# A down projection whose hidden tiles are taken in chunks of six, eight and eight instead of eight, eight and six

## What is computed

```python
    hf = rms_norm(x, g_ffn)
    x = x + (jax.nn.silu(hf @ w_gate) * (hf @ w_up)) @ w_down
y_prompt = rms_norm(xp, g_final)
y_sample = rms_norm(xs, g_final)
```

## Time and profile before

| | |
|---|---|
| median of three runs | 803.87 us (803.01, 804.04, 803.87) |
| profiled execution | 803.4 us |
| its span, first to last instruction | 801.4 us |
| TensorE matmuls, busy | 783.0 us |
| VectorE, busy | 570.8 us |
| ScalarE, busy | 454.3 us |
| GpSimd, busy | 450.8 us |
| granted TensorE clock, mean share of full | 0.996 |

### The profile page before, as it was taken

How to read it: one execution, slowest core, us unless ns; L and a number is a source line. 1 busy time by engine, 2 the same in 40 slices (tenths; PEclk the granted TensorE clock), 3 DMA queues, 4 the chain that set the end, 5 groups by cost and what they waited for, 6 DMA issues and landing times.

```text
span 801.4 us, 16035 instructions
## 1 busy us (share of the span) xinstructions
PE 783.0 (98%) x5731; PEld 744.6 (93%) x5731; DVE 570.8 (71%) x1058; ACT 454.3 (57%) x865; POOL 450.8 (56%) x351
## 2 busy tenths in 40 slices
PE   7999999999999999999999999999999999999996
PEld 6987998888888999998899999999999999899996
DVE  6446477887779736457589777667676689998884
ACT  7462475666677334454465655555555566555464
POOL 3666873383213554741465454454674588889954
PEclk9999999999999999999999999999999999999998
DMA  8343432111025333340023233223332232232213
GB/s 258 115 124 108 155 92 79 36 34 41 28 79 176 128 106 105 106 132 28 18 96 107 97 106 105 71 86 105 105 105 66 91 106 84 76 106 88 81 45 119
DMA packets 26538, 75.93 MB, mean 95 GB/s; under 512 B 2912, under 2 KB 7464, under 8 KB 26344
## 3 DMA queue, kind: packets, MB, share of 16 engines
q1 hardware_dynamic: 25920, 74.28, 28.9%
q10 hardware_dynamic: 560, 0.88, 0.3%
HBM read 68.62 MB, written 6.53 MB: 94 GB/s over the span
## 4 chain that ended last, share of the span: by engine, by line
PE 86%; DVE 4%; issue 3%; ACT 3%; POOL 2%; DMA 1%; SPq 0%; POOLq 0%; DVEq 0%; ACTq 0%
PE ps L1179 13%; PE ps L652 13%; PE ps L1181 13%; PE ps L1180 13%; PE ps L654 12%; PE ps L653 12%; PE ps L814 2%; PE ps L832 2%; PE ps L670 1%; PE ps L1084 1%; ACT whi L1318 1%; DMA wraw<-w_front 1%; POOL wlo L2611 1%; PE ps L678 1%; PE ps L797 1%
## 5 line engine op out<-in xcount | busy, mean ns | idle before, releaser
L1318 ACT ACTIVATE whi<-wraw 128x512 fp32r<-128x512 f32 (+3 forms) x150 | 112.7, 755 | 91.5 <-PE ps L1181 43.4
L652 PE MATMUL ps<-hhi,whi 128*128 128x288 f32 x480 | 144.6, 301 | 5.9 <-DVE hlo L1877 5.8
L2762 POOL TENSOR_TENSOR wlo<-wraw,whi 128x512 fp32r<-128x512 f32 x63 | 86.2, 1381 | 106.5 <-ACT whi L1318 106.5
L654 PE MATMUL ps<-hlo,whi 128*128 128x288 f32 x480 | 143.0, 298 | 0.0
L653 PE MATMUL ps<-hhi,wlo 128*128 128x288 f32 x480 | 142.9, 298 | 0.0
L2611 POOL TENSOR_TENSOR wlo<-wraw,whi 128x256 fp32r<-128x256 f32 (+2 forms) x83 | 90.9, 1123 | 84.9 <-ACT whi L1318 84.7
L1179 PE MATMUL ps<-hhi,whi 128*128 128x288 f32 x380 | 112.2, 295 | 1.1 <-DVE xb L2480 0.6
L1180 PE MATMUL ps<-hhi,wlo 128*128 128x288 f32 x380 | 111.9, 295 | 0.0
L652 PEld LDWEIGHTS ps<-hhi,whi 128*128 128x128 f32 x480 | 91.2, 190 | 7.5 <-DVE hlo L1877 5.8
L1181 PE MATMUL ps<-hlo,whi 128*128 128x288 f32 x320 | 94.4, 295 | 0.0
L653 PEld LDWEIGHTS ps<-hhi,wlo 128*128 128x128 f32 x480 | 91.2, 190 | 0.2
(11 more groups left out here) (383 smaller groups left out, 2261.6 us busy)
## 6 DMA issues: line engine op xcount, KB each, us to landing
wraw<-w_ff SPq DMA_DIRECT2D x44, 512.0 KB, 4.1
wraw<-w_front SPq DMA_DIRECT2D x41, 512.0 KB, 3.7
wraw<-w_down SPq DMA_DIRECT2D x16, 512.0 KB, 4.1
wraw<-w_down SPq DMA_DIRECT2D x8, 384.0 KB, 3.5
wraw<-w_front SPq DMA_DIRECT2D x7, 384.0 KB, 3.8
xa<-x_t SPq DMA_DIRECT2D x8, 288.0 KB, 5.6
xs<-x_t SPq DMA_DIRECT2D x7, 288.0 KB, 5.7
out_y<-xb SPq DMA_DIRECT2D x5, 288.0 KB, 2.6
```

What stands on the lines that cost most here:

```text
L652: nc.tensor.matmul(out, lh, rh, start=start, stop=False)
L654: return nc.tensor.matmul(out, lh, rl, start=False, stop=stop)
L1318: return nc.scalar.activation(out, src, func, **kw)
L2762: g.tensor_tensor(w_operand(1, j), src, f(w_operand(0, j)), ALU.subtract).then_inc(g_lo, 1)
```

## The change

The chunks become 6, 8 and 8 tiles. Stage 0's weights are still prepared in blocks of 512 columns, of which 384 are the stage's own, so its load places each block of 384 columns at a distance of 512. The places of hidden operands (`D_HI`) and the uses that they wait for (`D_PLACE`) follow the new sizes, and so do the counts of scaled tiles (6, 14, 22). Squares at the end lie in tiles 6 and up. `hidden_scaled(20)` goes from VectorE's stage 1 to GpSimd, behind `down_rest(1, 1)`. The last column sums of the second half take tile 13, then `sqacc`, then tile 12. Core of the diff:

```diff
@@ -43,7 +43,7 @@
 B_FRONT = 49
 BLOCK_COLS = [768 if b < 4 or b in B_UQ else 1024 for b in range(B_FRONT)]
 BLOCK_AT = [sum(BLOCK_COLS[:b]) for b in range(B_FRONT + 1)]
-DOWN_K = (8, 8, 6)
+DOWN_K = (6, 8, 8)
 
 
 TICKS = 80
@@ -467,19 +467,19 @@
 
         D_SRC = [turns(c, True) for c in range(3)]
         D_LO = [turns(c, False) for c in range(3)]
-        D_HI = [{0: pb[:, :, :], 2: hlo[:, 0:4, x_low], 1: th[0][:, :, :], 4: tl[0][:, :, :], 3: hhi[:, 4:8, x_low],
-                 5: hlo[:, 4:8, x_low], 6: th[2][:, :, :]},
+        D_HI = [{0: pb[:, 0:3, :], 2: hlo[:, 0:3, x_low], 1: th[0][:, 0:3, :], 4: tl[0][:, 0:3, :], 3: hhi[:, 4:7, x_low],
+                 5: hlo[:, 4:7, x_low], 6: th[2][:, 0:3, :]},
                 {0: hhi[:, 0:4, x_high], 2: hlo[:, 0:4, x_high], 1: hhi[:, 4:8, x_high], 4: hlo[:, 4:8, x_high],
                  3: pb[:, :, :], 5: hlo[:, 0:4, x_low], 6: pa[:, :, :]},
-                {0: tl[0][:, 0:3, :], 2: hhi[:, 4:7, x_low], 1: hlo[:, 4:7, x_low], 4: th[2][:, 0:3, :], 3: hidlo[:, 0:3, x_low],
-                 5: hidlo[:, 4:7, x_low], 6: hidlo[:, 0:3, x_high]}]
+                {0: tl[0][:, :, :], 2: hhi[:, 4:8, x_low], 1: hlo[:, 4:8, x_low], 4: th[2][:, :, :], 3: hidlo[:, 0:4, x_low],
+                 5: hidlo[:, 4:6, :].rearrange("p k (h t) -> p (k h) t", h=2), 6: hidlo[:, 0:4, x_high]}]
         T_PLACE = [{5: ff_used(G, 0)}, {4: ff_used(G, 4), 2: ff_used(G, 3), 5: ff_used(G, 3)}, {4: used_at(3, 4), 2: used_at(3, 5), 5: used_at(3, 1)}]
         D_PLACE = [{2: ff_used(G, 0), 1: ff_used(G, 2), 4: ff_used(G, 2), 3: ff_used(G, 1), 5: ff_used(G, 1),
                     6: ff_used(G, 4)},
                    {0: ff_used(G, 5), 2: ff_used(G, 5), 1: ff_used(G, 6), 4: ff_used(G, 6), 3: used_at(3, 0), 5: used_at(3, 2),
                     6: used_at(3, 2)},
-                   {0: used_at(3, 4), 2: used_at(3, 3), 1: used_at(3, 5), 4: used_at(3, 6), 3: used_at(3, 0), 5: used_at(3, 1),
-                    6: used_at(3, 3)}]
+                   {0: used_at(3, 4), 2: used_at(3, 3), 1: used_at(3, 5), 4: used_at(3, 6), 3: used_at(3, 1), 5: used_at(3, 6),
+                    6: used_at(3, 6)}]
 
         def down_w(s):
 
@@ -501,7 +501,8 @@
         def down_raw(s, r, k):
 
             w = down_w(s)
-            return w_raw((NW + s, None))[:, r, w * k:w * k + w]
+            at = 512 * k if s == 0 else w * k
+            return w_raw((NW + s, None))[:, r, at:at + w]
 
         def down_loaded(eng, s):
 
@@ -1280,8 +1281,8 @@
 
             def last_columns(half):
 
-                sources = ((hidf[:, 15, :], e_sq, 4), (hidf[:, 14, :], e_sq, 4), (sqacc[:, 0:T], e_acc, 5)) if half == 0 else \
-                    ((sqacc[:, 0:T], e_acc, 7), (hidf[:, 15, :], e_sq, 6), (hidf[:, 14, :], e_sq, 7))
+                sources = ((hidf[:, 13, :], e_sq, 4), (hidf[:, 12, :], e_sq, 4), (sqacc[:, 0:T], e_acc, 5)) if half == 0 else \
+                    ((hidf[:, 13, :], e_sq, 6), (sqacc[:, 0:T], e_acc, 7), (hidf[:, 12, :], e_sq, 7))
                 for n0, (source, signal, count) in enumerate(sources):
                     after(pe, signal, count)
                     for n in range(LAST_N):
@@ -1713,7 +1714,7 @@
                 if j in TURNS:
                     turns_made(act, c, TURNS[j])
                 else:
-                    act.wait_ge(s_hsc, (8, 16, 22)[c])
+                    act.wait_ge(s_hsc, (6, 14, 22)[c])
                 if j in D_PLACE[c]:
                     act.wait_ge(g_used, D_PLACE[c][j])
                 activation(D_HI[c][j], D_SRC[c][j]).then_inc(h_hi[0], 1)
@@ -1771,7 +1772,7 @@
 
             def pair_squares(b):
                 after(act, d_vec, vec_at(8 + b, "x7"))
-                activation(hidf[:, 8 + 2 * b:10 + 2 * b, :], xb[:, 2 * b:2 * b + 2, :], ACT.Square).then_inc(e_sq[0], 1)
+                activation(hidf[:, 6 + 2 * b:8 + 2 * b, :], xb[:, 2 * b:2 * b + 2, :], ACT.Square).then_inc(e_sq[0], 1)
 
             def gains_on(m, cols):
                 activation(xb[:, m, cols], xb[:, m, cols], scale=gains[:, G_FIN + m:G_FIN + m + 1]).then_inc(s_xg, 1)
@@ -1779,7 +1780,7 @@
             def half_squares(m0, m1, cols, names):
                 for s, name in names:
                     after(act, d_vec, vec_at(s, name))
-                activation(hidf[:, 8 + m0:8 + m1, cols], xb[:, m0:m1, cols], ACT.Square).then_inc(e_sq[0], 1)
+                activation(hidf[:, 6 + m0:6 + m1, cols], xb[:, m0:m1, cols], ACT.Square).then_inc(e_sq[0], 1)
 
             window((0, None))
             with act.Fori(0, NW // 2 - 2) as i:
@@ -1837,7 +1838,7 @@
 
             def last_row(half):
                 act.wait_ge(n_row, 7 + 2 * half)
-                activation(hidf[:, 8 + half, 0:HT], ps[:, 1 + 3 * half, 0:HT]).then_inc(n_rs, 1)
+                activation(hidf[:, 6 + half, 0:HT], ps[:, 1 + 3 * half, 0:HT]).then_inc(n_rs, 1)
 
             last_root(0)
             half_squares(4, 6, x_high, ((LA, "x7"),))
@@ -2539,7 +2540,6 @@
                 x6(s)
                 if s == 1:
                     hidden_turn(1, 2)
-                    hidden_scaled(20)
                 elif s == 2:
                     hidden_low(1, 4)
                 elif s == 3:
@@ -2765,7 +2765,7 @@
 
                 src = D_SRC[c]
                 if j == 4:
-                    pool.wait_ge(s_hsc, (8, 16, 22)[c])
+                    pool.wait_ge(s_hsc, (6, 14, 22)[c])
                     a, b = quarter(hidf, c, 0, x_high), src[0]
                 elif j == 3:
                     turns_made(pool, c, 1)
@@ -2807,7 +2807,7 @@
                     g.tensor_tensor(lo[:, 0:2, :], src[:, 0:2, :], hi[:, 0:2, :], ALU.subtract)
                 op_low(0, p)
                 if n == NW:
-                    g.tensor_tensor(lo[:, 2:4, :], src[:, 2:4, :], hi[:, 2:4, :], ALU.subtract).then_inc(h_lopool[0], 1)
+                    g.tensor_tensor(lo[:, 2:D_KN[0], :], src[:, 2:D_KN[0], :], hi[:, 2:D_KN[0], :], ALU.subtract).then_inc(h_lopool[0], 1)
                 op_low(1, p)
                 if n in TURN_AT:
                     hidden_turn(0, TURN_AT[n])
@@ -2829,11 +2829,11 @@
                 after(pool, e_sq, count)
                 if nth_ == 1:
                     pool.wait_ge(s_hsc, 22)
-                    other = hidf[:, 9, cols]
+                    other = hidf[:, 7, cols]
                 else:
                     after(pool, e_acc, nth_ - 1)
                     other = sqacc[:, cols]
-                g.tensor_tensor(sqacc[:, cols], other, hidf[:, 8 + m, cols], ALU.add).then_inc(e_acc[0], 1)
+                g.tensor_tensor(sqacc[:, cols], other, hidf[:, 6 + m, cols], ALU.add).then_inc(e_acc[0], 1)
 
             MADE_AT = {(0, 0): ((hidden_low, 0, 6),), (1, 1): ((hidden_turn, 1, 4), (hidden_turn, 1, 3)),
                        (2, 1): ((hidden_turn, 1, 5), (hidden_low, 1, 0)), (3, 1): ((hidden_low, 1, 2), (hidden_low, 1, 1)),
@@ -2844,6 +2844,8 @@
             for s in range(LA):
                 for j in (0, 1, 5):
                     down_rest(s + 1, j)
+                    if (s, j) == (0, 1):
+                        hidden_scaled(20)
                     for work, c, k in MADE_AT.get((s, j), ()):
                         work(c, k)
             whole = slice(0, T)
@@ -2863,7 +2865,7 @@
                 pool.wait_ge(n_rs, 6 + half)
                 pool.wait_ge(s_xg, 8 + 2 * half)
                 g.tensor_tensor(xb[:, m0:8, cc], xb[:, m0:8, cc],
-                                hidf[:, 8 + half, 0:HT].unsqueeze(1).to_broadcast([128, 8 - m0, HT]), ALU.mult).then_inc(s_yp, 1)
+                                hidf[:, 6 + half, 0:HT].unsqueeze(1).to_broadcast([128, 8 - m0, HT]), ALU.mult).then_inc(s_yp, 1)
 
             outputs(0, 6)
             outputs(1, 6)
@@ -3017,7 +3019,11 @@
                 at = 2 * sum(down_w(n) * 2 for n in range(s))
                 w = 2 * down_w(s)
                 for r in range(2):
-                    sp.dma_start(w_raw((NW + s, None))[:, r, 0:w], i_["w_down"][:, at + w * r:at + w * r + w])\
+                    dst, src = w_raw((NW + s, None))[:, r, 0:w], i_["w_down"][:, at + w * r:at + w * r + w]
+                    if s == 0:
+                        dst = w_raw((NW, None))[:, r, :].rearrange("p (k n) -> p k n", k=2)[:, :, 0:down_w(0)]
+                        src = src.rearrange("p (k n) -> p k n", k=2)
+                    sp.dma_start(dst, src)\
                         .then_inc(w_load[(NW + s) % 2], 16)
 
             sp.wait_ge(r_x, 8 + 8)
```

## The result

| | before | changed |
|---|---|---|
| median, first comparison (4 executions each) | 803.46 us | 813.77 us (807.72, 809.09, 818.44, 818.94) |
| ratio, 95% interval | | 1.0128 [1.0095, 1.0161] |
| profiled execution / its span | 803.4 / 801.4 us | 807.72 / 805.7 us |
| granted TensorE clock, mean | 0.996 | 0.997 |

Slower, and the median lies 0.3 us above the forecast range. The four times are two pairs, and their median is a point between them at which nothing ran; the changed kernel's two later comparisons, of twelve and six executions, both have a median of 808.48 us. All comparisons together hold 22 executions of the changed kernel: 17 between 807.38 and 809.84 us (median 808.4) and 5 between 818.06 and 819.14. Of 77 of the kernel before, 71 lie between 802 and 805, five between 806 and 810, one at 949, and none between 810 and 820.

The account below looks back on a forecast made before the run. TensorE, busy 98% of the span, was taken as the bound, with VectorE nearly so in the first chunk. Terms +3.5 + 2.9 - 0.8 - 0.2 = +5.4 us gave a median of 809.3 us, range 804.0 to 813.5.

Parts of the forecast that it names:

- the two squeezes: VectorE short of time in stages 0 to 4, +3.5 us, and GpSimd in stages 5 to 8, +2.9; chance 0.55.
- (0,0) and the wait behind it: Product 0 of down stage 0, now shorter: its 0.4 us are waited away behind it, for ScalarE's copy.
- stages 0 to 4: Down projection's first stages: VectorE's work exceeds TensorE's matmul time, so stalls become 6.8 us against 3.7.
- stages 5 to 8: GpSimd's wider turns and rests for chunk 2 come late: 3.0 us more stall, term +2.9 us.
- stages 8 to 11: Last down stages: VectorE has time to spare, the stall at 778.61 goes, longer last product covers column sums; -0.8 us.
- order of the last column sums: End of the second half: tile 13, ready earlier, goes before the accumulated squares; -0.2 us, at worst 0.
- Loads: Weight loads of the down stages: later or in smaller pieces, yet in time; 0, the first up to +1 us.
- 2 us of waits taken up: Ahead of GpSimd's turn 3 of chunk 1: some 2 us of its waits for ScalarE would be absorbed.
- the step on the 3.40 us rest: VectorE's SBUF rest at 746.25, which cost 0.5 us at 750.63, can recur or be covered; taken as covered.
- the port compounds it: Rival: GpSimd overtakes VectorE's product 6 rests in three or four stages, 0.5 to 1 us each; +8.5, 812.4 us, chance 0.15.
- Faster: Rival: moving the row product ends stalls in stages 0 to 4, GpSimd has slack in 6 to 8; -4.8, 799.1 us, chance 0.1.
- Only one squeeze counts: Rival: GpSimd's lateness in stages 6 to 8 is absorbed, or the first chunk costs little; +2.6, 806.5 us, chance 0.15.

## Why the prediction was right and wrong

**Right: the direction and the two squeezes.** By its own terms, for the profiled usual execution (the 0.4 us of (0,0), part of the first term's 3.5, stands alone):

| term | forecast | measured |
|---|---|---|
| (0,0) and the wait behind it | +0.4 | -0.18 |
| all ahead of that | 0 | -0.57 |
| stages 0 to 4 | +3.1 | +2.9 |
| stages 5 to 8 | +2.9 | +3.2 |
| stages 8 to 11 (measured from stage 9 on) | -0.8 | -0.9 |
| order of the last column sums | -0.2 | -0.2 |
| sum | +5.4 | +4.3 |

Stage 0 starts at 662.25 against 663.40, 1.15 us earlier. 0.4 of it is the three matmuls that (0,0) no longer has; the wait behind it, for ScalarE's copy, did not grow by them as forecast but went from 0.5 to 0.3. The other 0.57 differs from execution to execution: in the third profile of the same kernel (0,0) starts 0.65 us later, and the span is 806.4, 5.0 above the kernel before's, which is the distance of the two usual medians (808.4 and 803.4). The row of stages 8 to 11 is 33.95 us from 762.55 to 796.50 against 26.9 from 765.10 to 792.0, less the 8.0 us of matmuls that moved there. The term for stages 5 to 8 has a slip that happened to help: with 3.0 us of stall after, and the 0.5 of before taken as covered, it comes to +2.5 and not +2.9. Loads: ScalarE waits 10.8 us for them in all from 655 us on, but TensorE never does; 0 was right. GpSimd shows no idle time between its turns of chunk 2 and the last hidden rest, as the prediction's sign asks.

**Right, by steps, and in part by luck.** Turn (1,3) was to end at 682.5, and ended at 682.57; (2,4) was to start near 685.5, and did at 685.27; stage 5 near 715.4, and did at 714.05. The first two agree by luck, for the forecast had stage 0 start at 663.4 and it started at 662.25: counted from there the turn came at 20.3 us and not 19.1, (2,4) at 23.0 and not 22.1, so the stalls up to (2,4) are 3.8 us where 2.9 were forecast. Stage 5, at 51.8 against 52.0, is right on that count too. TensorE waits for GpSimd first at (7,0), forecast 1.0 us late, measured 0.95. For (8,0) and (9,0) 1.8 and 3.0 us, counting all before, were forecast; measured are 0.95 + 1.2 = 2.15 and 3.45.

**Partly wrong: how the first chunk's stalls lie.** Stages 0 to 3 were to take 10 to 11 us each. They took 10.35, 8.45, 11.25 and 9.50: stage 1 has no stall inside it, with 7.7 us of VectorE work in 8.45. Under 9.3 was to be a sign of being wrong, and VectorE was to be over 90% busy, where stage 2 has 9.56 of 11.25. The sum was right, the spread not. And the working charged the moved product 1.4 us on the way to turn (1,3). The later placing showed that it sits in a pause that ScalarE sets, so the turn depends on neither the 1.4 nor, in full, the "2 us of waits taken up": with the pause kept, the turn came 1.2 us later than worked out.

**Wrong: the median, by the step on the 3.40 us rest.** The prediction's sentence was that the rest from SBUF that took 3.40 us at 746.25 "can recur or be covered; I take it as covered". That step has no upper bound, and needed one. The row showed an instruction whose kin with a PSUM sum take 0.68 us passed over by the two GpSimd instructions at 746.86. The row behind them, in GpSimd's timeline of the kernel before, says when that ended:

```profile
749.39 1.15 POOL L2826 TENSOR_TENSOR wlo<-wraw,whi 128x384 fp32r<-128x384 f32 x1 [0.29 <-ACT whi L1318]
```

GpSimd finished at 749.11 and paused, and the rest ended at 749.65, 0.54 us later, as the 13.44 us one ended 0.55 us behind GpSimd's last. So the kernel before already showed a rest held until GpSimd had nothing ready; there the run was short. The upper bound was in reach: GpSimd is busy 11.20 of 11.20 us in stage 6 and 11.01 of 11.30 in stage 7, so by estimate a whole stage, 11 us. The chunks then gave it 12.17 of 12.25 and 12.50 of 12.50. The rival "the port compounds it" named the mechanism but priced it at 0.5 to 1 us in each of several stages. In the execution that was traced it is one rest, that of product 6 of stage 7, the very one that had taken 3.40 us: 13.44 us, a stall of 10.45, and the times 10 us longer come in 5 of 22 executions. With two groups of times 10 us apart, a median of few executions can fall between them, and the range should have held that: its top of 813.5 was the end of the smooth cases. That the first four fell two and two was chance (at 5 in 22, two or more of four are long about once in five times); with the medians of the later comparisons, 808.48, the same prediction would have been in its range with the same step missing.

**The other rivals.** "Faster" was right that the product made VectorE late in stage 2: moved alone it gives 2.15 us. It failed at the point it gave itself, the first chunk's load (48.8 us of VectorE work in stages 0 to 4, where the prediction had 49.9, for 45.2 of matmuls): the chunks cost 7 us. "Only one squeeze counts" fell with both terms measured.

**Open.** Why VectorE gets its turn behind the first GpSimd instruction in most executions and in others never, until GpSimd has nothing ready: the two traces differ by 0.03 us in the start of its instruction (738.36, 738.39), and no run varied that alone. Whether the chip matters is open as well. A first chunk of six with less hidden work in it was not tried. The 806 to 810 and the 949 and 2508 us executions of the kernels with the old chunks were not traced. Of the seven long executions without waits one was traced.

## What to carry to other kernels

Shorter stages for TensorE are no gain where the partners' work per stage does not shrink with them: divide each engine's work per stage by the stage's matmul time before choosing a chunk, for each engine that makes operands. And where a VectorE instruction reads only SBUF beside a long unbroken run of GpSimd, bound its time by all that GpSimd has ready, not by one instruction, and look in the trace for a rest that ends when GpSimd pauses. Where times fall into two groups, take a profile of each.

## What the hardware showed that was not expected

- A VectorE rest of 128x512 with both operands in SBUF took 13.44 us (1.55 in the usual execution) while ten GpSimd instructions ran back to back, and ended 0.55 us after the last. The Trainium skill, "SBUF — State Buffer", section "SBUF: two separate sides", has the loser blocked while the other's instruction holds the port; the trace agrees for the 1.55 us of the usual execution, and shows here that the next instruction of the same engine can go first again, nine times, though VectorE's had begun before them.
- The profile counts that time as busy: VectorE is "busy" 9.27 of 9.80 us with two instructions. A busy share near 100% with far fewer instructions than the engine otherwise runs in such a stretch can be a wait.
- TensorE's granted clock fell from 1.00 to 0.51 during the 10.45 us stall and stayed there for 4.7 us after it, 2.1 us of added time. With the product back on VectorE a stall of 3.13 us was enough: the clock stood at 0.50 behind it, 1.4 us of added time. The stretches with the usual stalls, up to 1.8 us, stand at 1.00.
